# Gate stores in eight pieces, and the two ends of the expert stage, in a one-core decoder layer

## The reference, cut to what matters

```
h = rmsnorm(x, ffn_norm_w)
q = h @ w_query                        # 8 heads x 2 halves x 128
s = q . sub_keys                       # 128 keys a half
top 16 of each half -> 256 candidates -> top 16: expert_idx, gate = softmax(best)
a = gelu(h . expert_down[idx])         # 128 experts a token (8 heads x 16)
x = x + sum(gate * a * expert_up[idx])
out = rmsnorm(x, final_norm_w)
```

## Time and profile before

| | us |
|---|---|
| median of 3 runs | 1718.87 (1717.88 to 1720.74) |
| the profiled execution | 1719.09 |
| its span in the trace | 1717.4 |
| PE busy in the span | 1666.0 (97%) |
| PE weight loads busy | 1494.0 (87%) |
| DVE, POOL, ACT busy | 1136.0, 835.2, 672.5 |
| mean traffic | 247 GB/s |

### The profile page before, as it was taken

How to read it: one execution, slowest core, us unless ns; L and a number is a source line. 1 busy time by engine, 2 the same in 40 slices (tenths; PEclk the granted TensorE clock), 3 DMA queues, 4 the chain that set the end, 5 groups by cost and what they waited for, 6 DMA issues and landing times.

```text
span 1717.4 us, 26045 instructions
## 1 busy us (share of the span) xinstructions
PE 1666.0 (97%) x8905; PEld 1494.0 (87%) x8905; DVE 1136.0 (66%) x2253; ACT 672.5 (39%) x972; POOL 835.2 (49%) x483
## 2 busy tenths in 40 slices
PE   7999999999999999999999999998999999999998
PEld 5788787868999999999999999997887878878886
DVE  4154552031295999796898888205878777878787
ACT  5342433342334343434444444333333333333333
POOL 3462374312255878786576666554333333434230
PEclk9999999999999999999999999999999999999999
DMA  4222243213635988887899999749999999999993
GB/s 172 89 96 74 74 148 123 86 50 101 207 133 189 297 285 276 285 286 255 312 322 324 332 339 348 263 146 335 321 355 335 352 330 352 339 348 351 342 347 146
DMA packets 148395, 423.38 MB, mean 247 GB/s; under 512 B 14320, under 2 KB 67568, under 8 KB 147440
## 3 DMA queue, kind: packets, MB, share of 16 engines
q1 hardware_dynamic: 93472, 237.53, 41.2%
q0 software_dynamic: 36864, 134.23, 21.8%
q10 hardware_dynamic: 18000, 50.89, 7.5%
HBM read 373.32 MB, written 49.28 MB: 246 GB/s over the span
## 4 chain that ended last, share of the span: by engine, by line
PE 58%; issue 20%; DMA 9%; POOL 9%; DVE 2%; ACT 1%; SPq 0%; POOLq 0%; ACTq 0%; DVEq 0%
PE psum L1136 18%; PE psum L1137 18%; PE psum L1138 18%; POOL w_low L367 9%; DMA arena<-down_rows,kept 4%; DMA arena<-hid_dram 4%; PE psum L1403 3%; DMA arena<-up_in 1%; DVE arena L1028 1%; PE psum L1389 1%; DMA kept<-down_in 1%; ACT w_high L459 0%; DVE arena L926 0%; DVE arena L1022 0%; DVE wgt_low L1067 0%
## 5 line engine op out<-in xcount | busy, mean ns | idle before, releaser
L367 POOL TENSOR_TENSOR w_low<-kept,w_high 128x1024 fp32r<-128x1024 f32 x212 | 517.4, 2443 | 481.2 <-ACT w_high L459 480.1
L1136 PE MATMUL psum<-hT_high,w_high 128*128 128x384 f32 (+1 forms) x1408 | 492.2, 350 | 7.3 <-POOL w_low L367 4.1
L1138 PE MATMUL psum<-hT_high,w_low 128*128 128x384 f32 (+1 forms) x1408 | 485.3, 345 | 0.0
L1137 PE MATMUL psum<-hT_low,w_high 128*128 128x384 f32 (+1 forms) x1408 | 485.1, 345 | 0.0
L1136 PE MATMUL psum<-up_high,wgt_high 128*128 128x512 f32 x768 | 301.2, 392 | 10.4 <-DVE wgt_low L1067 10.4
L1137 PE MATMUL psum<-up_low,wgt_high 128*128 128x512 f32 x768 | 299.8, 390 | 0.0
L1138 PE MATMUL psum<-up_high,wgt_low 128*128 128x512 f32 x768 | 299.7, 390 | 0.0
L459 ACT ACTIVATE w_high<-kept 128x1024 fp32r<-128x1024 f32 x212 | 224.1, 1058 | 192.5 <-DMA kept<-front_w 71.7
L1136 PEld LDWEIGHTS psum<-hT_high,w_high 128*128 128x128 f32 x1408 | 264.8, 188 | 19.2 <-issue 4.5
L1138 PEld LDWEIGHTS psum<-hT_high,w_low 128*128 128x128 f32 x1408 | 264.6, 188 | 10.3
L1137 PEld LDWEIGHTS psum<-hT_low,w_high 128*128 128x128 f32 x1408 | 264.9, 188 | 9.8 <-issue 0.5
(11 more groups left out here) (197 smaller groups left out, 1982.6 us busy)
## 6 DMA issues: line engine op xcount, KB each, us to landing
kept<-down_in SPq DMA_DIRECT2D x128, 512.0 KB
arena<-up_in SPq DMA_DIRECT2D x128, 512.0 KB
kept<-front_w SPq DMA_DIRECT2D x100, 512.0 KB
gate_dram<-arena ACTq DMA_DIRECT2D x6, 4096.0 KB, 15.9
arena<-gate_dram SPq DMA_DIRECT2D x32, 768.0 KB, 8.8
hid_dram<-arena ACTq DMA_DIRECT2D x112, 192.0 KB
arena<-hid_dram SPq DMA_DIRECT2D x112, 192.0 KB
kept<-x_in ACTq DMA_DIRECT2D x4, 512.0 KB, 5.0
```

Of the source, the lines that this page charges most:

```text
L367: nc.gpsimd.tensor_tensor(w_low[:, s, :], ring[:, s, :], w_hi[:, s, :].bitcast(F32), ALU.subtract).then_inc(low_ready, 1)
L1136: nc.tensor.matmul(out, lhs[0], rhs[0], start=first, stop=False)
L1137: nc.tensor.matmul(out, lhs[0], rhs[1], start=False, stop=False)
L1138: return nc.tensor.matmul(out, lhs[1], rhs[0], start=False, stop=last)
```

## The change

Four things are changed, and what follows from them.

1. **Gate stores.** The store of a chunk is cut into 8 pieces of 512 KB (16 of the 128 rows of `stage` for each partition), and these are issued on ACT's queue during the steps of the next chunk: one after each of its first six steps, two after the seventh, none after the eighth. The last chunk's eight pieces are issued together. The waits on `stored` count the pieces.
2. **The step from down to up stage.** ACT makes up_high and wgt_high of block 0 right after the gelu of the down stage's fourth last block, and those of block 1 after the second last gelu. The sparse tile's own gelu (`gel3`) moves to behind the third last. On DVE `sparse_up` runs one block later, and w3 is made after block 0's wgt_low. PE's waits on the last two gelus (banks 4 and 5) are made exact.
3. **Start.** x and `vec` (after its second tile) go first in SP's queue and the weight blocks follow without a wait; ACT issues nothing there. DVE waits for `vec` only ahead of `norm_gain`, and scales tiles 2 and 3 whole instead of in halves. PE makes three products of constants while x is loaded.
4. **End.** The last two blocks are computed together, bank by bank, so that the six banks are finished one after the other. DVE's order of `accumulate` and `final` follows from that; the last tile's square, scaling and store are done in halves.

```diff
+PIECES = 8
+PIECES_AT = (1, 1, 1, 1, 1, 1, 2, 0)
...
+            for t in range(NT):
+                sp.dma_start(x[:, t, :], x_in[t * P:(t + 1) * P, :]).then_inc(ld_x[t], 16)
+                if t == 1:
+                    sp.dma_start(vec, vecs_in).then_inc(ld_vec, 16)
             for s in range(RING):
-                sp.wait_ge(ld_x[1 + 2 * (s // 2)], 16)
                 load_block(s, s)
...
-            for n, t in enumerate(TILES_LAST):
+            for n, t in enumerate(TILES_LAST[:-1]):
                 sp.wait_ge(fin_y, n + 1)
                 sp.dma_start(out[t * P:(t + 1) * P, :], fin_out[:, t, :]).then_inc(out_stored, 16)
-            sp.wait_ge(out_stored, 16 * NT)
+            t = TILES_LAST[-1]
+            for c in range(2):
+                sp.wait_ge(fin_y, NT + c)
+                sp.dma_start(out[t * P:(t + 1) * P, c * 512:(c + 1) * 512], fin_out[:, t, c * 512:(c + 1) * 512])\
+                    .then_inc(out_stored, 16)
+            sp.wait_ge(out_stored, 16 * (NT + 1))
...
-            for t in range(NT):
-                act.dma_start(x[:, t, :], x_in[t * P:(t + 1) * P, :]).then_inc(ld_x[t], 16)
-            act.dma_start(vec, vecs_in).then_inc(ld_vec, 16)
...
+            def store_gates(c, q):
+                rows = P // PIECES
+                act.dma_start(gate_dram[:, c, q * rows * CH:(q + 1) * rows * CH],
+                              stage[:, c % 2, q * rows:(q + 1) * rows, :].rearrange("p i n -> p (i n)"))\
+                    .then_inc(stored[c % 2], 16)
+
             for n in range(STEPS):
...
                 if k == 0 and c >= 2:
-                    act.wait_ge(stored[c % 2], 16 * (c // 2))
+                    act.wait_ge(stored[c % 2], 16 * PIECES * (c // 2))
...
-                if k == CH // TB - 1:
-                    act.wait_ge(gate_out, 2 * (n + 1) + 3)
-                    act.dma_start(gate_dram[:, c, :], stage[:, c % 2].rearrange("p i n -> p (i n)"))\
-                        .then_inc(stored[c % 2], 16)
-
+                if c:
+                    if k == 0:
+                        act.wait_ge(gate_out, 2 * n + 3)
+                    for q in range(sum(PIECES_AT[:k]), sum(PIECES_AT[:k + 1])):
+                        store_gates(c - 1, q)
+
+            act.wait_ge(gate_out, 2 * STEPS + 3)
+            for q in range(PIECES):
+                store_gates(DCH - 1, q)
...
                 nc.scalar.activation(hid_kept[j], psum[:, 4 + i % 2, 0:DN], ACT.Gelu).then_inc(gelu_out, 1)
-                if i >= NK - 3:
-                    high_up(i - NK + 3, i - NK + 3, 16)
-            act.wait_ge(dot_done, SLOTS)
-            nc.scalar.activation(gel3, dot3, ACT.Gelu).then_inc(gel3_ready, 1)
-            high_up(3, 3, 16)
-            for s in range(4):
+                if i == NK - 4:
+                    high_up(0, 0, 16)
+                    weight_high(0, 0)
+                if i == NK - 3:
+                    act.wait_ge(dot_done, SLOTS)
+                    nc.scalar.activation(gel3, dot3, ACT.Gelu).then_inc(gel3_ready, 1)
+                if i == NK - 2:
+                    high_up(1, 1, 16)
+                    weight_high(1, 1)
+            for s in range(2, 4):
+                high_up(s, s, 16)
                 weight_high(s, s)
...
+                elif n < NT - 1:
+                    act.wait_ge(x_added, 2 * t + 2)
                 else:
+                    act.wait_ge(x_added, 2 * t + 1)
+                    step(nc.scalar.activation(junk[:, 0:512], x[:, t, 0:512], ACT.Square, accum_out=ss[:, NT:NT + 1]))
+                    step(nc.scalar.activation(ms[:, NT:NT + 1], ss[:, NT:NT + 1], ACT.Identity, scale=1.0 / D, bias=eps))
                     act.wait_ge(x_added, 2 * t + 2)
...
+            norm_rows(mixn)
             dve.wait_ge(ld_vec, 16)
-            norm_rows(mixn)
             norm_gain(mixn)
...
             weigh(0, 0, 0, 16, SPILL + 3, hid_kept[0])
-            dve.wait_ge(gel3_ready, 1)
-            step(nc.vector.tensor_tensor(w3, gel3, gate3, ALU.mult))
             for s in range(15):
                 low_up(s, s % 4)
                 weigh(s + 1, s + 1, (s + 1) // 4, 16, SPILL + s + 4, hid_kept[s + 1])
                 weight_low(s, s % 4)
-                sparse_up(s, s % 8, 16 * (s // 8 + 1), s if s else None)
+                if s == 0:
+                    dve.wait_ge(gel3_ready, 1)
+                    step(nc.vector.tensor_tensor(w3, gel3, gate3, ALU.mult))
+                else:
+                    sparse_up(s - 1, (s - 1) % 8, 16 * ((s - 1) // 8 + 1), s - 1 if s > 1 else None)
...
-            for n, t in enumerate(TILES_LAST):
-                if t != ST:
-                    accumulate(2 * t)
-                    accumulate(2 * t + 1)
-                if n != 1:
-                    final(max(n - 1, 0), TILES_LAST[max(n - 1, 0)])
-            final(NT - 1, TILES_LAST[-1])
+            final(0, ST)
+            for n, t in enumerate(TILES_LAST[1:]):
+                accumulate(2 * t)
+                accumulate(2 * t + 1)
+                if n:
+                    final(n, TILES_LAST[n])
+            final(NT - 1, TILES_LAST[-1], (slice(0, 512), slice(512, D)))
...
+            for _ in range(3):
+                nc.tensor.matmul(psum[:, 3, :], ident, reset, start=True, stop=True)
             turned_columns(mixn, 0, 0)
...
                     if first and o in (4, 5):
-                        pe.wait_ge(gelu_out, NK - 1 + o - 4 + 1)
+                        pe.wait_ge(gelu_out, NK + o - 3)
...
-            for s in range(4):
-                second_product(NK - 4 + s, s, last=(s == 3))
+            for s in range(2):
+                second_product(NK - 4 + s, s)
+            pe.wait_ge(up_low, NK)
+            pe.wait_ge(w_ready, NK)
+            for o in range(2 * DT):
+                for s in (2, 3):
+                    ins = three(psum[:, o, :], [w[:, s, (o // 2) * P:(o // 2 + 1) * P] for w in wgt_half],
+                                [u[:, s, (o % 2) * 512:(o % 2 + 1) * 512] for u in up_half], False, s == 3)
+                ins.then_inc(out_done, 1)
```

39 lines of the change are left out of this document (21 added, 18 removed).

## The result

Twenty runs of each kernel, side by side: the changed kernel takes 1721.67 us in the median (1714.68 to 1728.26), the one before 1717.34 (1710.55 to 1724.31). The ratio is 1.0027, with a 95% interval of 1.0014 to 1.0040, so the change costs 4.6 us, give or take 2.2. The prediction was 1708.9, faster. Its profiled execution took 1720.06 us with a span of 1718.3.

What follows compares the result with a forecast made beforehand. PE was taken as the bound, so only its gaps, half-clock passes and both ends could be won. Terms 5.0 + 0.8 + 2.5 + 1.7 = 10.0 us gave 1709.1 profiled, 1708.9 median; 8 in 10 range 1704.5 to 1713.5.

Steps and rivals of the forecast that it cites:

- Gate stores, the five within the stage: Gate steps: five stores spread in pieces over the next chunk's steps win 5.0 us; bounds 1 and 5.8.
- the sum of shares: Gate steps: DMA share with spread stores, 0.78 + 0.22 = 1.0, fitting with 3% to spare.
- no room: Gate steps: DMA engines have no room, pieces wait in each step, 4 us less gain, 1712.9; 14%.
- The last store: Behind the gate steps: eight issues take some 3 us; w_high(+2) comes 3 us later, still half a microsecond ahead of need.
- the slower rival: Gate stores: each piece's issue blocks ACT, 40 pieces eat the gain or make the kernel slower, 1724.9; 3%.
- Transition: Down to up stage: PE stalls 3.5 before the last down block, clock falls, net gain 0.8 us; bounds 0.8 and 3.2.
- the third rival: Up stage takes the lead back: PE begins sooner after the gathers' start, stalls of 3 us in all, 1711.9; 6%.
- if not, some tenths: Up block 2: ready 7.9 us after PE's end, needed at 8.2, just in time; otherwise some tenths lost.
- Start: Kernel start: earlier x, whole-tile scaling and a warmed clock, first product at about 13.7; gain 2.5 us in all.
- the bound of 0.5: Kernel start: lower bound of the gain in us, if x ends no earlier and the clock is as before.
- End: Kernel end: banks finished one by one, last tile in halves, gain 1.7 us; bounds -0.9 and 2.3.
- The price below nothing: Kernel end: if Identity wanted a table, 1.28 us for a load and another back, term at -0.9.

Runs made afterwards that it cites:

- e6: Kernel before with only the stores changed: five chunks in pieces during the next chunk's steps, the last chunk in one whole store; 0.9989 (0.9975 to 1.0002).
- e4: Changed kernel with three edits: last chunk in one store, weight_high(0) behind the second last gelu, start as before; 0.9954 of the kernel before (0.9936 to 0.9971).
- e16: Kernel before with the stores alone exactly as changed, the last chunk's eight pieces issued together; 0.9991 (0.9974 to 1.0009).
- e3: Changed kernel with the start of before: x in ACT's queue, scaling by halves, no constant products; 1.0017 of the kernel before (0.9999 to 1.0035).
- e2: Changed kernel with weight_high(0) moved from behind the down stage's fourth last gelu to behind its second last; 0.9969 of the kernel before (0.9945 to 0.9992).
- after: The changed kernel with all four parts, and its profile; 1.0027 of the kernel before, 1721.67 us in the median, 1720.06 in the profiled execution.
- e10: e4 with the last chunk's store in eight pieces, one behind each of the next eight gelus; 0.9931 of the kernel before (0.9911 to 0.9952), 1706.05 us.
- e1: Changed kernel with the last chunk's gates in one store of 4096 KB instead of eight pieces; 0.9998 of the kernel before (0.9984 to 1.0013).
- e11: e4 with the edits of both e9 and e10; 0.9928 of the kernel before (0.9903 to 0.9953).
- e17: Changed kernel with only the edits of e2 and e10, new start and end kept; 0.9931 of the kernel before (0.9904 to 0.9959), 1707.3 us.
- e7: Changed kernel with the edits of e1 and e2, the new start kept; 0.9958 of the kernel before (0.9942 to 0.9974).
- e8: e4 with the end of before too: last two blocks one after the other, last tile whole; 0.9958 of the kernel before (0.9942 to 0.9973).
- e9: e4 with the up stage's gathers ramped, four in flight at first and one more with every second; 0.9963 of the kernel before (0.9939 to 0.9987).
- e12: Kernel before with the mended transition alone, weight_high(0) behind the second last gelu as in e2; 0.9978 (0.9962 to 0.9994).
- e18: e17 with the transition of before: first up blocks' weights behind the last gelu, sparse_up not shifted; 0.9951 of the kernel before (0.9932 to 0.9969).
- e14: Kernel before with the new end alone; 0.9990 (0.9969 to 1.0011).

## Why the prediction was wrong

**Gate stores, the five within the stage: right.** Predicted 5.0; gate is 4.3 to 5.7 shorter than in the two profiles of before. The DMA engines had the room that the sum of shares left open: eight undisturbed steps of the changed kernel (917.58 to 965.15) move 341 GB/s at a share of 0.96; the prediction asked for 341 and reckoned with 352 for a full share. So the rival "no room" fell. (The 334 GB/s that it calls the mean of both stretches is a chunk's traffic over its time with the stall; the two rows together give 326.) What the five chunks win is in part lost behind them, though: e6, which changes them alone, is 1.9 us faster (2.3 either way) and not 5, and burst is 0.6 to 3.2 longer in all profiles with pieces and a whole last store: PE's gap behind that store is 2.06 in e6, with the half clock behind it, and 2.95 in e4, against 1.45 to 1.97 with six whole stores. Why the weight block lands later there stays open. The Trainium skill's rule of 1 MiB or more per transfer ("DMA: Bandwidth & Descriptors", section "Bandwidth") isn't what decides here: eight 512 KB pieces in a row reach 415 GB/s at a share of 1.05, the 4096 KB store had 412 at 1.02.

**The last store: the first step that failed.** The prediction put it so: "The last store keeps its burst. Its eight issues take some 3 us, and w_high(+2), which lies behind them, then comes 3 us later than before, still half a microsecond ahead of need." It multiplied the issue of one by eight. Measured, the eight take 8.45 (8.48, 8.54 and 9.07 in the profiles of e16, e3 and e2), `w_high` comes too late by 4.49 of PE's time, and the clock falls behind that gap. Burst is 28.9 (after, e16), and 29.8 and 29.9 in e2 and e3, where the half clock lasts longer (6.8 us instead of 3.4); before it was 24.5, so the term is 4.4 on the wrong side. Where no store disturbs it, it is 22.6 (e10), and the 6.3 between are the gap of 4.49 and eleven passes at half clock of 0.147 more each (1096.03 to 1099.55), 1.6, together 6.1. By the ratios of after and e1 the eight issues cost 5.0, with some 3 us of uncertainty.

The eight issues grow from 0.34 to 1.5, and from the fourth on each takes 1.11 to 1.52, about as long as a piece of 524 KB needs at 415 GB/s, 1.26. This fits an issue that is held up by the transfers ahead of it in ACT's own row of issues: all eight are 4.19 MB, which at 415 GB/s take 10.1 us. Full engines alone don't do it. SP's loads at 1087.56 and 1091.72, between ACT's slow issues, take 0.33 each, and ACT's single pieces in e10 take 0.45 also at 1092.96, in a stretch (1092 to 1094) with a share of 1.02. This is the mechanism of the slower rival ("a piece's issue blocks ACT"), but at one place, not in forty.

Whether it takes the full engines as well was not tried: no run issues eight in a row while the engines are free. What is shown is that one issue per block costs nothing (0.34 to 0.45 each, no gap), and that this wins more than a whole store: burst falls from 25.8 (e4) to 22.6, and the three kernels with it (e10, e11, e17) stand at 0.9930 in the mean, the four with the whole store and the mended transition (e4, e7 to e9) at 0.9958, 4.8 us more, with 2.9 of uncertainty; e10 against e4 alone, 3.9, has 4.6. The 3.2 of burst between them is a weight block that lands late behind 4 MB. The prediction had counted the last store's stall as not to be had.

The trace of the kernel before could have warned of it. There SP issues the first up blocks and gate loads in a row at the end of the down stage (1154.4 to 1163.6), and their issues grow in the same way: 0.34, 0.42, 0.43 and 0.57 for four of 512 KB, then 0.65, 0.74, 2.81 and 2.80 for four of 768 KB.

**Transition: the mechanism right, the net a miss.** The stall is 4.17 (predicted 3.5): from the gelu ahead of it to DVE's product of the gates it took 1167.88 - 1160.31 = 7.57 instead of 7.19, and POOL's split 2.70 instead of 2.39, which make the 0.7; the clock fell as forecast (0.64 and 0.68 of two stretches). Trans is 73.3 against 73.2: +0.1 instead of -0.8. Moving the wait behind the last `w_high` (e2) takes 7.0 off it.

But the up stage gives part back, a term that the forecast put at nothing: the second step that failed. This is the third rival, held for 6%: "the up stage takes the lead back". In the 13 profiles in which PE enters the up stage without a pause, up is 529.4 in the mean; in the 7 with the old pause, 525.0; the difference is 4.4, with a standard error of 1.6. Of it 2.7 are PE's gaps (6.6 us against 3.9 in the mean), and 1.2 is the clock, which is at half for 3.4 us against 1.0. The 13 have a first gap for `wgt_low` within 40 us of the stage's start: four (e4, e8, e10, e12) at up block 2, 0.9 to 1.3 us long, which the prediction weighed ("if not, some tenths"), and nine at up block 8, 35 to 38 us in and 1.9 to 5.1 long. In the 7 the first gap behind the pause comes 64 us in (e18, 0.95) or later. It is a mean over profiles whose kernels differ in other things too, and it scatters: the profile of after has the gap (2.01) but an up of 527.4, no longer than before's. The ratios agree within their wide uncertainty: e12 won 3.8 (2.7 either way) of 6.9, and the transition as changed, which starts the up stage without a pause but wins nothing at its place, is 1.0018 alone, 3.1 us slower (3.3 either way), 6.9 behind e12.

What the traces show of the cause is what the rival named. With the pause POOL's first gather of the up stage is issued 4.06 us before PE's first product, without it 0.44 after it; from 10 to 35 us into the stage the 13 then move 391 GB/s in the mean at a share of 1.01, the 7 move 363 at 0.97, and the gap of the nine stands right behind these 25 us. So there the blocks are late behind a stretch in which the DMA engines are full. Which of the transfers would have to give way stays open; the ramp of the gathers (e9) didn't cure it.

**Start: missed.** 2.5 predicted, from a first product at 13.7. It came at 15.71, and over the profiles with the new start between 14.4 and 16.2, with the old one between 15.0 and 15.7. Of its three steps one held: with whole tiles it is 5.47 from ACT's square of the last tile to the first product (10.24 to 15.71), before it was 6.33 (8.92 to 15.25), so 0.9 is won where "about 1" was forecast. That "its last tile should come about 0.5 earlier" failed: that square starts 1.3 later in the changed kernel, and at 8.97 to 10.67 over the seven profiles with the new start, against 8.81 to 9.38 over the other 13. `vec` now stands ahead of the third tile in the same queue, and the two late tiles follow it. DVE, which scales from 7.22 on, waits 3.35 for the second pair.

The clock failed too. The constant products run until 8.2, and the clock is full over 8 to 12 (1.00); but PE has only eight transposes then and idles 3.44 before the next ones, and over 15 to 20 the clock is at half (0.50). Passes are long until 20.97. All seven profiles with the new start begin the first product with long passes (0.76 to 0.77); of the 13 with the old one five (the second profile of before, e3, e9, e14 and e16) begin it with short ones (0.47), without any constant products. Alone the start gave 0.9984, which is the predicted 2.5 us as well as nothing; after against e3, e7 against e4 and e17 against e10 gave 1.7 us lost, 0.7 lost and nothing. The four together, weighted by their uncertainty, are 0.5 us won, with 1.9 either way: the bound of 0.5 would have been the better value.

**End: right in kind, 0.5 too large.** Tail 7.26 instead of 8.43: 1.2 for 1.7. `final` of the shared tile runs at 1705.83, because the last sparse rows are added late, and the accumulations behind it start at 1707.03 as a queue of four. The lag is the price of the transition, which runs `sparse_up` one block later: with the new end and `sparse_up` as before the tail is 6.32 (e14) and 6.34 (e18), 2.1 less than before, and with both it is 7.1 to 7.3. The price below nothing, a table load for Identity, did not come up: ACT's one load there is at 1699.72, ahead of the squares. The ratios can't show a term of this size.

**The sum.** Predicted -10.0, measured +4.6 (2.2 either way): 14.6 to explain. Against their predicted values the last burst is +4.4 to 5, the transition +0.8, the up stage +4.4 (a mean over profiles, not the one of after), the start +2.0 to 2.5 and the end +0.5. They make 12.1 to 13.2, and the rest is within the uncertainty. The gate steps were shorter by 4.3 to 5.7 us, more than the 2 us that the prediction set as its test for the stage, and yet the forecast failed: the test guarded the term that held.

## What to carry to other kernels

Don't price n issues in a row as n times one: what stands behind them on the issuing engine can be late by nearly as long as the transfers take (here 8.45 of 10.1 us). If a store is cut in pieces, spread all of them, the last chunk's above all, one to a step with slack (e10 and e17, which do, beat the kernel before by 0.7%), and put no wait for DRAM ahead of the split of the next weight block. When a seam is shortened, read the next 50 us as well: here a good part of the 6.9 us won at the seam, about half by e12, was paid back by late loads.

## What the chip showed unasked

- Issue of 512 KB stores from ACT: 0.34 us alone, 0.45 behind a gelu's store in the spread version, 1.04 for two, 8.45 for eight in a row, the last ones 1.5 each; a single one of 4096 KB takes 0.34, and SP's loads in the midst of the eight take 0.33. Here one large transfer held the issuing engine less than its pieces did.
- Gaps of 4.49 and 4.17 us of PE were both followed by the half clock (0.66 over 1095 to 1100, 0.64 over 1170 to 1175), adding 1.6 us (eleven passes) to the first and 2.6 (the block's 24 passes take 1179.53 - 1172.77 = 6.76, at full clock 4.16) to the second. Of shorter gaps some were followed by it and some not: 2.01 at 1214.55 was (0.66 over 1215 to 1220), 2.70 at 462.58 in the same profile wasn't (1.00 over 465 to 470); 3.03 in e1 was (0.66 over 1105 to 1110), 2.95 at 1104.89 in e4 wasn't (1.00 over the same stretch).
- Constant products from 3.42 to 8.22 were followed by the full clock (1.00 over 8 to 12); behind a pause of 3.44 that ended at 12.79 the first products had long passes again (0.63 to 0.78) until 20.97.
- One kernel on one core varies by several us between executions: 1710.55 to 1724.31 over 20 runs of the kernel before, and 4.2 ahead of the first gelu in its two profiles. With 12 runs of a kernel the interval was mostly some 0.18% either way, with 20 of each 0.13%.
